# Sixteen odd weight units of the first layer's second branch: from SyncE's queue to ScalarE's

## The reference

```python
proj = x @ w_in
h_a, c_a, b_a, z_a, qkv, z_b, beta_raw, a_raw = jnp.split(proj, cuts, axis=-1)
y_a = b_a * causal_depthwise_conv(c_a * h_a, conv_a_w) * jax.nn.silu(z_a)      # first branch
qkv = jax.nn.silu(causal_depthwise_conv(qkv, conv_b_w))                        # second branch
q, k = l2_normalize(q), l2_normalize(k)
o = gated_delta_rule(q, k, v, g, beta)                                         # 8 heads of 128, chunks of 64
o = rms_norm(o, gdn_norm_g) * jax.nn.silu(z_b)
return jnp.concatenate([y_a, o], axis=-1) @ w_out
```

## Time and profile before

| | |
|---|---|
| median of 3 runs | 945.38 us (945.13 to 948.46) |
| the profiled execution | 948.59 us, of it 946.8 us span |
| PE busy | 917.7 us (97%) |
| ACT, DVE, POOL busy | 504.1, 474.1, 673.7 us |
| granted TensorE clock, mean | 0.991 of full speed |
| moved by the DMA queue of SP, of ACT | 140.64 MB, 4.24 MB |

### The profile page before, as it was taken

How to read it: one execution, slowest core, us unless ns; L and a number is a source line. 1 busy time by engine, 2 the same in 40 slices (tenths; PEclk the granted TensorE clock), 3 DMA queues, 4 the chain that set the end, 5 groups by cost and what they waited for, 6 DMA issues and landing times.

```text
span 946.8 us, 19454 instructions
## 1 busy us (share of the span) xinstructions
PE 917.7 (97%) x7694; PEld 847.7 (90%) x7694; DVE 474.1 (50%) x975; ACT 504.1 (53%) x711; POOL 673.7 (71%) x486
## 2 busy tenths in 40 slices
PE   5899899999999999999999999999999999999997
PEld 5899899998998788999999999888898799998886
DVE  3448855468543163566777767726646352221004
ACT  3675343474234565656675666555567365554341
POOL 3787655655656687976767767677798569889983
PEclk9999899999999999999999999999999999999999
DMA  5769356556534655754444553455663247666641
GB/s 181 204 205 175 97 133 113 137 125 112 135 114 117 211 172 157 209 168 144 131 142 145 157 153 126 147 180 175 190 201 113 89 131 222 190 191 200 203 133 45
DMA packets 133299, 146.12 MB, mean 154 GB/s; under 512 B 11022, under 2 KB 100056, under 8 KB 133208
## 3 DMA queue, kind: packets, MB, share of 16 engines
q1 hardware_dynamic: 131224, 140.64, 52.1%
q10 hardware_dynamic: 1984, 4.24, 1.3%
HBM read 143.81 MB, written 1.05 MB: 153 GB/s over the span
## 4 chain that ended last, share of the span: by engine, by line
PE 80%; DVE 7%; POOL 4%; issue 3%; ACT 3%; DMA 3%; SPq 1%; DVEq 0%; ACTq 0%; POOLq 0%
PE dense L565 22%; PE dense L567 21%; PE dense L566 21%; DMA raw<-in_w_in_even_dram 3%; PE bank L940 2%; POOL wlo L540 2%; POOL wlo L539 2%; PE bank L835 1%; PE bank L831 1%; PE bank L850 1%; ACT whi L1197 1%; DVE cv L1787 1%; PE dense L634 1%; PE bank L948 1%; PE bank L969 1%
## 5 line engine op out<-in xcount | busy, mean ns | idle before, releaser
L540 POOL TENSOR_TENSOR wlo<-raw,whi 128x512 fp32r<-128x512 f32 (+1 forms) x263 | 411.6, 1571 | 25.6 <-ACT whi L1197 25.5
L539 POOL TENSOR_TENSOR wlo<-raw,whi 128x512 fp32r<-128x512 f32 x199 | 258.5, 1299 | 217.2 <-ACT whi L1197 213.8
L1197 ACT ACTIVATE whi<-raw 128x1024 fp32r<-128x1024 f32 x264 | 275.6, 1058 | 246.6 <-PE dense L567 196.4
L565 PE MATMUL dense<-x_hi,whi 128*128 128x256 f32 x1232 | 356.4, 289 | 7.6 <-POOL wlo L534 4.8
L566 PE MATMUL dense<-x_lo,whi 128*128 128x256 f32 x1232 | 346.6, 281 | 0.0
L567 PE MATMUL dense<-x_hi,wlo 128*128 128x256 f32 x1232 | 346.3, 281 | 0.0
L565 PEld LDWEIGHTS dense<-x_hi,whi 128*128 128x128 f32 x1232 | 234.8, 191 | 14.0 <-issue 7.3
L566 PEld LDWEIGHTS dense<-x_lo,whi 128*128 128x128 f32 x1232 | 236.1, 192 | 0.6 <-issue 0.2
L567 PEld LDWEIGHTS dense<-x_hi,wlo 128*128 128x128 f32 x1232 | 235.3, 191 | 0.0
L565 PE MATMUL dense<-whi,ya_hi 128*128 128x512 f32 x192 | 77.6, 404 | 1.0 <-issue 0.8
L567 PE MATMUL dense<-whi,ya_lo 128*128 128x512 f32 x192 | 75.0, 391 | 0.0
(11 more groups left out here) (336 smaller groups left out, 1411.7 us busy)
## 6 DMA issues: line engine op xcount, KB each, us to landing
raw<-in_w_in_odd_dram SPq DMA_DIRECT2D x64, 512.0 KB, 3.8
raw<-in_w_in_even_dram SPq DMA_DIRECT2D x32, 512.0 KB, 7.2
raw<-in_w_in_even_dram SPq DMA_DIRECT2D x64, 256.0 KB, 4.3
raw<-in_mlp_w_up_dram SPq DMA_DIRECT2D x32, 512.0 KB, 3.9
raw<-in_mlp_w_down_dram SPq DMA_DIRECT2D x32, 512.0 KB, 4.5
raw<-in_w_out_even_dram SPq DMA_DIRECT2D x16, 512.0 KB, 3.7
raw<-in_w_pl_gate_dram SPq DMA_DIRECT2D x16, 512.0 KB, 4.3
raw<-in_w_out_odd_dram SPq DMA_DIRECT2D x16, 512.0 KB, 3.9
```

The costliest lines, as they stand in the source:

```text
L539: pool.tensor_tensor(wlo[:, slot, 0:half], unit_slot(u)[:, 0:half], whi[:, slot, 0:half].bitcast(F32), ALU.subtract)
L540: pool.tensor_tensor(wlo[:, slot, first:2 * half], unit_slot(u)[:, first:2 * half], whi[:, slot, first:2 * half].bitcast(F32), ALU.subtrac ...
L565: pe.matmul(out_, lh, rh, start=start, stop=False, skip_group_check=True)
L1197: act.activation(whi[:, u % NSPL, :], unit_slot(u), ACT.Copy).then_inc(hi_done, 1)
```

## The change

The sixteen odd units from 1 to 31 leave SP's queue, with their waits, and are issued by ACT. Units 1, 3 and 5 go out at ACT's start, before and behind the first table load. Each of the other thirteen is issued behind the rounding of the unit four before it, in `split_until`; it first waits for its slot as SP did (`lo_done` at least u - 5). SP issues the second half of x directly behind unit 0 (it was behind unit 1). The small loads ahead of the units 9, 11 and 13 stay in SP's queue and now have no wait of their own unit in front of them.

```diff
+SECOND_QUEUE = range(1, 32, 2)
...
             for u in range(SPLITS):
                 slot, v = u % NRAW, SWAPPED.get(u, u)
                 c, part = LOADS[v // 2], v % 2
-                if u == 2:
+                if u == 1:
                     load_x(1)
...
-                if u >= NRAW:
+                if u >= NRAW and u not in SECOND_QUEUE:
                     sp.wait_ge(lo_done, u - NRAW + 1)
...
+                if u in SECOND_QUEUE:
+                    continue
                 dst = raw[:, slot, :]
...
+            def load_unit(u):
+
+                slot, v = u % NRAW, SWAPPED.get(u, u)
+                if u >= NRAW:
+                    act.wait_ge(lo_done, u - NRAW + 1)
+                w = weights(LOADS[v // 2], v % 2)
+                act.dma_start(raw[:, slot, :].rearrange("p (k c) -> p k c", k=4), w).then_inc(raw_ready[slot], 16)
+
             def split_until(end):
...
                     act.activation(whi[:, u % NSPL, :], unit_slot(u), ACT.Copy).then_inc(hi_done, 1)
                     at["unit"] += 1
+                    if u + 4 >= NRAW and u + 4 in SECOND_QUEUE:
+                        load_unit(u + 4)
...
             act.dma_start(con[:, 0:C_UPTO], consts[:, 0:C_UPTO]).then_inc(consts_loaded, 16)
+            load_unit(1)
             tables(SILU_TABLES)
+            load_unit(3)
+            load_unit(5)
             take_hi(xf0, x_hi, 0, range(2))
```

## The result

| | before | after |
|---|---|---|
| median of 6 runs each, same series | 947.18 us (945.13 to 949.43) | 950.67 us (949.52 to 952.44) |
| ratio, with its 95% interval | | 1.0049 (1.0035 to 1.0064) |
| the profiled execution, its span | 948.59 us, 946.8 us | 951.56 us, 949.7 us |
| last weight unit rounded by ACT at | 924.5 us | 927.4 us |

The change makes the kernel slower. The medians differ by 3.5 us; the ratio, which is formed over the rounds and not from the two medians, gives 4.6 us (3.3 to 6.1). The forecast was 944.0 us.

What follows compares the result with a forecast made beforehand. PE, busy 97% of the span, was taken to bound the kernel, leaving only its early waits and low clock to win. -4.2 + 0.6 + 2.2 = -1.4 us on the median 945.4 us gave 944.0 us, range 940.5 to 950.0 us.

Steps and rivals of the forecast that it cites:

- What bounds the kernel: PE is busy 97% of the span; loading can win only where PE waits or runs at low clock, early on.
- Issue cost on ACT: Sixteen load issues on ACT, those with their wait already met running beside a rounding: costed at nothing.
- The start: Unit 1 in flight beside x's first half delays the tail of x: 0.6 us, bounds 0 and 1.9 us.
- low bound for the supply: Total rate unchanged, only the order changes; unit 4 comes as now, unit 6 gains: 2.6 less 0.6, 2.0 us.
- The supply: Second queue fills idle engines, units 3 to 8 arrive ahead of need; PE's later waits and low clock go: -4.2 us.
- rival B: Supply not faster, ACT's waits paid: +0.2 us, 945.6 us, or 947.2 us if the clock stays low; chance 0.20.
- The small loads: tail_w and gate rows go out on SP before unit 8, which is issued near 25 us, covered by 2 us.
- The new wait: ACT waits for POOL behind the roundings of units 15, 19 and 21, delaying the key norms: +2.2 us.
- Rival C: ACT's issue of unit 7's load near 19 us is held behind SP's: 947.6 to 951.2 us; chance 0.13.
- Rival D: Longer PE hole near 76 us brings the low clock for six microseconds: +1.6 us, 947.0 us; chance 0.10.
- The sum: Supply, start and new wait for the whole kernel: -4.2 + 0.6 + 2.2 = -1.4 us.

Runs made afterwards that it cites:

- the pair of late units: Start as in the kernel before, units 13 to 31 odd on ACT: 948.64 us, 1.0014; the same without 19, 23 and 25: 947.79 us, 1.0001.
- loop alone: Changed kernel with the start as before the change, only odd units 7 to 31 on ACT: 951.77 us, 1.0066 to the kernel before.

## Why the prediction was wrong, step by step

**What bounds the kernel.** Right as far as it goes: all that changed lies before 130 us.

**Issue cost on ACT: nothing.** Right: 0.37 us each beside a rounding. Where an issue had waited, it stood alone, and its 0.37 us is part of the hold, as counted.

**The start: +0.6 us.** This is the step that failed, in place and in size. In PE's waits it is 3.6 (unit 0) + 2.9 (x_lo) - 0.2 (x) = +6.3 us. I asked only whether unit 1's bytes would delay x. They did not: PE waits 4.8 us for x (5.0 us before). What is delayed is the rest of SP's queue. With 1, 3 and 5 in ACT's queue and half the engines given to it, unit 1 overtakes unit 0, the units 3 and 5, 1.0 MB, overtake unit 2, and unit 2 lands 6.9 us later. My low bound for the supply even says it ("units 3 and 5 are early, unit 4 then has the same bytes in front of it"), but I applied it to unit 4 and not to unit 2, which has bytes in front of it that it did not have before. Alone, with what its waits give back later already taken off, the start costs 2.6 us (1.1 to 3.9). It is unit 5 that does it: with 1 and 3 alone unit 2 is 2.5 us late, and no loss is seen beyond the interval.

**The supply: -4.2 us.** Right in size, wrong in its reason, so luck in part. Its four rows did vanish, 1.9 us of later low parts, 0.7 us of the gate and the low clock at 36 us, but in part because PE arrived later, not because the data came sooner: unit 4 lands at 24.4 us (23.8 us). The reason given, that the second queue fills the idle engines, was wrong for this kernel: 6.2 MB by 36 us both times, and a share of 0.57 from 14 to 24 us bought by 0.58 instead of 0.64 ahead of it. This is one half of rival B's sign (unit 4 at 24 us; the other, a share under 0.5 from 14 to 24 us, did not come). B stood at 0.20, with its price too low because its start term was. The rule of the Trainium skill that I had weighed and not followed, page "DMA: Bandwidth & Descriptors", section "Issuing engines are not separate DMA queues", is what happened here; the trace agrees for the changed kernel with 6.2 MB each. It is not the whole story: without unit 5 the same two queues moved 7.3 MB.

The share of the two queues, 0.68 and 0.67 MB from 2 to 8 us, is what I should have used. The Trainium skill states it too, in the same page, section "Queues, rings and completion order": each DMA engine takes turns between the queues that have work for it. The trace agrees with it, by those two numbers.

**The small loads.** I had them go out behind unit 6 and before unit 8. In the program they stand behind unit 8, and so they went (unit 8 at 25.52 us, tail_w at 25.93 us). That unit 8 was issued near 25 us as forecast is luck: not the small loads held it, but the slot of unit 2.

**The new wait: +2.2 us.** Right in its three places and in its size, 2.0 us (0.9 to 3.0). In the pair of late units vT, the third place, shifts by 2.7 us, where I had 2.2 us in all on ACT.

**Rival C** is refuted: no issue of ACT in the changed kernel took over 0.66 us, and one took 0.38 us beside SP's 10.80 us. What the Trainium skill says in "Perfetto Trace Analysis", section "DMA Instruction — HWDGE (DVE, Sync)", of a lock on the descriptor generator is not seen between SP and ACT here; the section names the sequencers of DVE and SyncE, and I had carried it over to ACT.

**Rival D** happened as well: the hole of 2.9 us near 76 us and 3.4 us of low clock behind it, where I had put 6 us. The stretch near 108 us shrank from 6.8 to 3.4 us in exchange, so these two cancel. (The 1.9 us by which I let the hole grow in this rival stood in no row; it was 2.0 us.)

**The sum.** In the profiled executions: -4.2 (supply) + 6.3 (start, forecast 0.6) + 2.0 (new wait, forecast 2.2) - 0.2 (VB) = +3.9 us, where I had -1.4. By the ratios, with the supply's rows inside the price of the start: 2.6 + 2.0 = +4.6 us. The range ended at 950.0 us; the start's real price lies behind it.

## What to carry to other kernels

A load put on a second queue does not only come earlier itself. Here the queues took turns (0.68 and 0.67 MB), so what the first queue held came later, and what waited for its slots later still. Write down for each item of the first queue how many bytes stand in front of it after the change, and compare with when it is wanted. Here one load of 512 KB decided: the units 1 and 3 were free, unit 5 on top cost 3.2 us. It is not the number that counts: the units 1 and 2 alone cost 1.9 us. Before paying for a wait, look at what would be late next: a longer wait at the very start (3 us here) can be paid out of waits that would have come later, and a wait named for one input (x_lo at 26.10 us) may hide another (unit 2's low part, 25.86 us) right behind it. Two rows merged into one in a timeline can hold a wait between them: show them one by one before calling an issue slow. A wait before an issue on a compute engine costs all that stands behind it, and POOL's ends and ACT's rows of before gave its size well.

No version beats the kernel before by more than its interval. The best are unit 1 alone (0.9992) and the changed kernel without 5, 19, 23 and 25 (0.9994).

## What was not expected of the hardware, and what is open

- Of two loads on two queues the one issued at 1.18 us landed at 8.4 us, and the one issued at 1.65 us behind half of x at 11.9 us. 0.47 us and the other queue's contents change the order of two 512 KB loads.
- An issue of SP can stand 10.80 us (loop alone) or 4.54 us (changed kernel) while one of ACT takes 0.38 or 0.37 us in the same stretch. So in these two cases the hold was SP's own and not of a part that ACT needed.
- Open: why the DMA engines are busy only about half of the time from 14 to 36 us, while loads are outstanding. With the small loads moved behind, the share stays at 0.47 from 14 to 24 us and rises to 0.65 from 24 to 36 us, without a gain in time (1.0003), so they explain a part at most. Why the total rises to 7.3 MB by 36 us without unit 5 and stays at 6.2 MB with it was not tried apart. The traces show that POOL frees the slot of unit 2 sooner, so that unit 8 is issued at 20.9 instead of 25.5 us; that this makes the difference is argued, not shown. With the units 1 and 3 alone on ACT it is 6.7 MB.
- Open: which low-clock stretches near 26, 36, 80, 108 and 230 us a run has. The run with x's second half first on the changed kernel had none before its end and took 948.0 us in its profiled execution, while the other seven runs of the same kernel took 948.5 to 954.5 us. Part of every difference of 1 us here may be that.
